# Two hybrid decoder layers: two weight column pairs exchanged, and the S5 states given to the output matmul as two VectorE products

## What is computed

```python
z = h @ w_in[l]                       # columns: s5_u, s5_gate, mla_cq, mla_ckv, mla_kr, ...
lam_bar = exp(lam * dt)
bu = einsum('blgh,gph->blgp', ug, b_bar)
state = linear_scan(lam_bar, bu)      # complex, along the tokens
y = einsum('blgp,ghp->blgh', state, c_c).real + d * ug
```

## Time and profile before

| | |
|---|---|
| runs before | 2877.06 us median of 3 (2876.66 to 2879.03) |
| profiled execution | 2878.85 us, span 2877.1 us, mean granted clock 0.993 |
| TensorE busy | 2804.0 us, 97% |
| VectorE busy | 1992.2 us, 69% |
| ScalarE busy | 1571.8 us, 55% |
| GpSimd busy | 745.6 us, 26% |
| HBM traffic | 183 GB/s over the span |

### The profile page before, as it was taken

How to read it: one execution, slowest core, us unless ns; L and a number is a source line. 1 busy time by engine, 2 the same in 40 slices (tenths; PEclk the granted TensorE clock), 3 DMA queues, 4 the chain that set the end, 5 groups by cost and what they waited for, 6 DMA issues and landing times.

```text
span 2877.1 us, 55833 instructions
## 1 busy us (share of the span) xinstructions
PE 2804.0 (97%) x16152; PEld 2410.4 (84%) x16152; DVE 1992.2 (69%) x3284; ACT 1571.8 (55%) x2812; POOL 745.6 (26%) x813
## 2 busy tenths in 40 slices
PE   6999999999999999999999999999999999999997
PEld 4878888888888888888877888888888888888886
DVE  8799999755555567555577999986555555755555
ACT  5555555655566565444455555556566555644443
POOL 3255555300001023111123545551001010411111
PEclk9999999999999999999999999999999999999998
DMA  6765656655555556777746565656555555577775
GB/s 225 227 186 177 184 175 183 180 166 159 165 156 169 164 149 201 217 210 209 206 142 190 173 186 175 186 173 179 166 155 168 163 154 157 168 211 217 209 210 175
DMA packets 276413, 522.65 MB, mean 182 GB/s; under 512 B 30913, under 2 KB 33873, under 8 KB 275281
## 3 DMA queue, kind: packets, MB, share of 16 engines
q1 hardware_dynamic: 257360, 477.13, 56.0%
q10 hardware_dynamic: 18944, 44.18, 4.8%
HBM read 508.60 MB, written 16.78 MB: 183 GB/s over the span
## 4 chain that ended last, share of the span: by engine, by line
PE 45%; DVE 2%; issue 2%; ACT 1%; POOL 0%; DVEq 0%; ACTq 0%; POOLq 0%
PE ps L294 26%; PE ps L293 13%; PE ps L443 1%; DVE w L973 1%; PE ps L326 1%; PE ps L456 0%; PE ps L452 0%; PE ps L296 0%; DVE zb L1512 0%; PE ps L337 0%; DVE yy L1042 0%; PE ps L304 0%; PE ps L465 0%; PE ps L464 0%; ACT w L590 0%
## 5 line engine op out<-in xcount | busy, mean ns | idle before, releaser
L294 PE MATMUL ps<-hb,w 128*128 128x512 f32 x5824 | 2053.0, 396 | 7.3 <-POOL hb L1542 6.1
L973 DVE TENSOR_TENSOR w<-raw,w 128x512 fp32r<-128x512 f32 x1760 | 1290.0, 740 | 789.6 <-ACT w L590 780.5
L590 ACT ACTIVATE w<-raw 128x512 fp32r<-128x512 f32 x1760 | 1092.9, 628 | 1035.3 <-PE ps L294 1034.3
L293 PE MATMUL ps<-hb,w 128*128 128x256 f32 x5690 | 1623.9, 285 | 13.8 <-DVE w L973 12.7
L294 PEld LDWEIGHTS ps<-hb,w 128*128 128x128 f32 x5824 | 1092.8, 188 | 251.4 <-issue 6.7
L293 PEld LDWEIGHTS ps<-hb,w 128*128 128x128 f32 x5690 | 1076.6, 189 | 57.0 <-DVE w L973 28.4
L294 PE MATMUL ps<-gl,w 128*128 128x512 f32 x640 | 226.7, 395 | 0.0
L1693 POOL TENSOR_TENSOR nf<-zb 128x256 f32 (+1 forms) x60 | 51.9, 864 | 537.2 <-DVE zb L1480 531.7
L294 PE MATMUL ps<-w,hb 128*128 128x512 f32 x512 | 179.1, 393 | 0.0
L293 PE MATMUL ps<-gl,w 128*128 128x256 f32 x560 | 156.6, 280 | 0.0
L1546 POOL TENSOR_TENSOR sx<-yl 128x256 f32<-128x256 f32 x16 | 15.6, 975 | 504.2 <-DVE yl L1346 504.2
(11 more groups left out here) (299 smaller groups left out, 2470.1 us busy)
## 6 DMA issues: line engine op xcount, KB each, us to landing
raw<-in_w SPq DMA_DIRECT2D x1763, 256.0 KB, 2.8
mlaw<-in_mlaw ACTq DMA_DIRECT2D x16, 768.0 KB, 4.2
mlaw<-in_mlaw ACTq DMA_DIRECT2D x16, 512.0 KB, 3.5
gate<-xres ACTq DMA_DIRECT2D x32, 256.0 KB, 4.3
xres<-zb ACTq DMA_DIRECT2D x32, 256.0 KB, 3.6
zb<-in_x SPq DMA_DIRECT2D x8, 512.0 KB, 7.3
xres<-in_x SPq DMA_DIRECT2D x4, 1024.0 KB, 6.5
s5w<-in_s5w ACTq DMA_DIRECT2D x16, 256.0 KB, 2.7
```

The costliest lines, as they stand in the source:

```text
L293: mm(acc[:, T:], a_lo, m_hi, start=False, stop=False, skip_group_check=True)
L294: last = mm(acc, a_hi, m_both, start=(k == 0), stop=(k == nk - 1), skip_group_check=True)
L590: A(w2[:, d, :, 0, :], raw[:, s, :, :], ACT.Copy).then_inc(hi_ready, 1)
L973: V.tensor_tensor(w2[:, d, :, 1, :], raw[:, s, :, :], w2[:, d, :, 0, :].bitcast(F), ALU.subtract).then_inc(w2_ready, 1)
```

## The change

It does three things.
1. The host orders the weight columns otherwise: pair 1 now holds the latents and the light half, pair 2 the second 512 S5 columns. `one=True` moves from pair 2 to pair 1 on TensorE and ScalarE, and VectorE gets the destinations of both pairs as an argument.
2. `s5_back` writes its product into a buffer of its own, `turned[j]`, (two in `gate`, two in a new tile `qki`, which also holds the former tiles qd, ki, ke and yl). `s5_state` and GpSimd's `back` go; `s5_back2` on VectorE, at step 8j + 6, makes the other product. VectorE takes over GpSimd's wait for `state_used` ahead of part 0.
3. `s5_out` multiplies `cprime` by both products and adds all four in PSUM: 16 matmuls instead of 8.

```diff
+        qki = sb("qki", [P, 4, T])
+        qd, ki, ke, yl = (qki[:, i, :] for i in range(4))
...
+        turned = (gate[:, 0, :, :], gate[:, 1, :, :], qki[:, 0:2, :], qki[:, 2:4, :])
...
                 pe.wait_ge(s5_done, it + 1)
-                pe.wait_ge(state_ready, it * 4 + 5)
+                pe.wait_ge(tab_used, it * 4 + 5)
+                pe.wait_ge(back_ready, it * 4 + 5)
                 for a in range(2):
-                    for j in range(4):
-                        last = mm(ps[32 * j:32 * j + 32, B_Y, 0:T], cprime[:, a, j, :], states[j][:, a, :],
-                                  start=(a == 0), stop=(a == 1), skip_group_check=True)
+                    for n, part in enumerate((states, turned)):
+                        for j in range(4):
+                            last = mm(ps[32 * j:32 * j + 32, B_Y, 0:T], cprime[:, a, j, :], part[j][:, a, :],
+                                      start=(a == 0 and n == 0), stop=(a == 1 and n == 1), skip_group_check=True)
...
-                pre_pair(1, {29: lambda: s5_in(l * G8, 0)})
-                pre_pair(2, s5_steps(l * G8, first=True), one=True)
+                pre_pair(1, {29: lambda: s5_in(l * G8, 0)}, one=True)
+                pre_pair(2, s5_steps(l * G8, first=True))
...
-                dve.wait_ge(state_ready, it * 4 + (j + 1))
+                dve.wait_ge(scanned, it * 8 + (2 * j + 1))
...
             def s5_back(it, j):
 
-                dve.wait_ge(scanned, it * 8 + (2 * j + 2))
-                V.tensor_tensor(yy[:, :, :], g2[:, ::-1, :], tab[:, 1:3, :], ALU.mult).then_inc(tab_used, 1)
-
-            def s5_state(it, j):
-                dve.wait_ge(tab_used, it * 4 + (j + 2))
-                dve.wait_ge(back_ready, it * 4 + (j + 2))
-                V.tensor_tensor(states[j][:, :, :], states[j][:, :, :], yy[:, :, :], ALU.add).then_inc(state_ready, 1)
+                dve.wait_ge(scanned, it * 8 + (2 * j + 3))
+                if j == 0:
+                    dve.wait_ge(state_used, it + 1)
+                V.tensor_tensor(turned[j], g2[:, ::-1, :], tab[:, 1:3, :], ALU.mult).then_inc(tab_used, 1)
+
+            def s5_back2(it, j):
+                V.tensor_tensor(states[j][:, :, :], g2[:, :, :], tab[:, 0:1, :].to_broadcast([P, 2, T]),
+                                ALU.mult).then_inc(back_ready, 1)
...
-                    for d, f in ((1, s5_rotate), (2, s5_rotate2), (3, s5_sum), (4, s5_scan), (5, s5_back), (7, s5_state)):
+                    for d, f in ((1, s5_rotate), (2, s5_rotate2), (3, s5_sum), (4, s5_scan), (5, s5_back), (6, s5_back2)):
...
-                pre_pair(2, s5_steps(l * G8, 0, first=True), one=True)
+                pre_pair(2, s5_steps(l * G8, 0, first=True),
+                         dst=(zb[:, Z_S5 + 4:Z_S5 + 6, :], zb[:, Z_S5 + 6:Z_S5 + 8, :]))
...
-            def back(it, j):
-
-                pool.wait_ge(scanned, it * 8 + (2 * j + 2))
-                if j == 0:
-                    pool.wait_ge(state_used, it + 1)
-                G.tensor_tensor(states[j][:, :, :], g2[:, :, :], tab[:, 0:1, :].to_broadcast([P, 2, T]),
-                                ALU.mult).then_inc(back_ready, 1)
...
                 turns(it, 1)
                 s5_cprime(it)
-                back(it, 0)
                 turns(it, 2)
-                back(it, 1)
                 turns(it, 3)
-                back(it, 2)
...
-                back(it, 3)
...
-    pre = np.concatenate([s5u, cq[:, :CC], kr, glr, pad, qk, lruu, cq[:, CC:], ckv, gv[:, :3 * CC]], axis=1)
+    pre = np.concatenate([s5u[:, :2 * CC], cq[:, :CC], kr, glr, pad, s5u[:, 2 * CC:], qk, lruu, cq[:, CC:], ckv, gv[:, :3 * CC]], axis=1)
```

More of the change, by code:

```diff
@@ L110, in trunk @@
         us = sb("us", [P, T])
-        yl = sb("yl", [P, T])
         kv = sb("kv", [P, 2, T])
@@ L119, in trunk @@
         lg = sb("lg", [P, 2, T])
-        qd = sb("qd", [P, T])
-        ki = sb("ki", [P, T])
-        ke = sb("ke", [P, T])
+        qki = sb("qki", [P, 4, T])
+        qd, ki, ke, yl = (qki[:, i, :] for i in range(4))
         attm = sb("attm", [P, 2, P])
@@ L173, in trunk @@
         cprime_ready, nf_ready, tab_ready = sem("cprime_ready"), sem("nf_ready"), sem("tab_ready")
-        bu_ready, bu_read, tab_used, state_ready, state_used = (sem("bu_ready"), sem("bu_read"), sem("tab_used"),
-                                                                sem("state_ready"), sem("state_used"))
+        bu_ready, bu_read, tab_used, state_used = (sem("bu_ready"), sem("bu_read"), sem("tab_used"),
+                                                                sem("state_used"))
         xc_ready, ri_ready, lru_act, yl_ready, yl_squared = (sem("xc_ready"), sem("ri_ready"), sem("lru_act"),
@@ L697, in _ @@
                 pre_pair(1, {0: [lam_exponent], 2: [turn_sines], 25: [lambda: s5_inputs(l * G8, 0)],
-                             31: [lambda: s5_tables(l * G8, 0)]})
+                             31: [lambda: s5_tables(l * G8, 0)]}, one=True)
                 own.restart()
-                pre_pair(2, s5_steps(l * G8, 0), one=True)
+                pre_pair(2, s5_steps(l * G8, 0))
                 own.restart()
@@ L1077, in _ @@
             dve.sem_inc(s5_done, 1)
-            dve.sem_inc(state_ready, 1)
+            dve.sem_inc(scanned, 1)
+            dve.sem_inc(back_ready, 1)
             C1 = 6.28125
@@ L1251, in _, with pre_pair @@
                 own.restart()
-                def pre_pair(i, steps, one=False):
+                def pre_pair(i, steps, dst=None):
                     for c in range(CH_PAIR):
@@ L1259, in pre_pair @@
                             h = c // CH_HALF
[L1260 to L1265, removed]
+                            z = zb[:, bass.ds(i * 4 + 2 * h, 2), :] if dst is None else dst[h]
+                            evac(h_l + (i * 2 + h), h, z, z.shape[1])
+                pre_pair(1, {0: [s5_turns], 4: [s5_scale], 6: [s5_scale2], 14: [lru_softplus]},
+                         dst=(zb[:, Z_LATENT[0]:Z_LATENT[0] + 2, :], kg.unsqueeze(1)))
                 own.restart()
-                pre_pair(2, s5_steps(l * G8, 0, first=True), one=True)
+                pre_pair(2, s5_steps(l * G8, 0, first=True),
+                         dst=(zb[:, Z_S5 + 4:Z_S5 + 6, :], zb[:, Z_S5 + 6:Z_S5 + 8, :]))
                 own.restart()
@@ L1536, in _ @@
             own.restart()
-            pool.sem_inc(back_ready, 1)
             def split_lo(k, count, dst=hb):
```

## The result

The changed kernel takes **2884.58 us** (median of 10 runs, 2883.81 to 2885.42) against 2877.22 us before (10 runs, 2876.07 to 2879.03): +7.4 us, a ratio of 1.0025, 95% interval 1.0017 to 1.0034. By that interval it is slower, where I had forecast 2875.0 us and a range up to 2881. The profiled execution took 2883.92 us (span 2882.1); the one of before lay 1.6 us above its median, so the two traces differ by 5.1 us only.

What follows compares the result with a forecast made beforehand. TensorE was taken to bound the kernel, with its waits for VectorE's low parts. The terms -20.4 + 3.0 + 1.0 + 14.3 = -2.1 us, against the median 2877.06 us, gave 2875.0 us, range 2869 to 2881.

Steps and rivals of the forecast that it cites:

- What bounds the kernel: TensorE, busy 97% of the span, waiting 13.2 us for VectorE's low parts; other engines' time counts only where TensorE waits.
- The pairs exchanged, and the new light half: Moving the light half (16 one-tile weight chunks) to pair 1 saves 20.4 us; stalls and loads there cost 3.0 and 1.0.
- the stalls: In pair 1's light half, low parts late behind VectorE's softplus chain: two stalls, 0.85 and 0.45 us; +3.0 us, two layers.
- the loads: In pair 1's light half, weight loads late, partly behind the first layer's 1 MB copy of x: +1.0 us, between 0 and 4.
- The rival of a light half that starves on loads: Pair 1's second half held up by raw loads, losing the old 10 us again: 2891 us; chance 0.10.
- the 358 GB/s of the prediction: HBM-to-core limit from the Trainium skill: 0.73 us a chunk, light half 0.5 us late by bandwidth alone; sum unchanged.
- Eight more matmuls: s5_out going from 8 to 16 matmuls adds four slots, 0.89 us, for each of 16 groups: +14.3 us on TensorE.
- On the path that is 0 us: Moving GpSimd's product to VectorE saves VectorE about 54 us and GpSimd some 120, but gains nothing on the path.
- the forecast "same": Whole kernel: -2.1 us, to 2875.0 us, within the 5.8 us that a measurement can't tell from no change; chance 0.57.
- The waits moved: ScalarE's tables wait for VectorE's step 6, about as early or earlier; VectorE's low parts behind its wait for state_used are safe.
- The one for a slower end: The rival that pair 1's light half starves on loads: 2891 us; chance 0.10.
- The one for dearer matmuls: Rival at s5_out: a gap up to 0.33 us a group between product sets, 5 us, 2880 us; slower only above +8, 0.04.

Runs made afterwards that it cites:

- the exchange alone: The kernel before with only the light half moved from pair 2 to pair 1 and the matching host column order: 2861.81 us, ratio 0.9943.
- the squares held back: The changed kernel, but GpSimd waits for the layer's last S5 product before it begins the squares of the latents: 2878.48 us, ratio 0.9999 to the kernel before.
- the cleared version: The exchange alone, with softplus moved to the middle stage and the third and fourth 1 MB copies of x issued 16 loads later: 2859.11 us, ratio 0.9936.
- the products alone: The kernel before with only the two separate products and 16 output matmuls, pairs not exchanged: 2895.91 us, ratio 1.0062.
- the doubled s5_out: The kernel before with each of s5_out's 8 matmuls issued twice, nothing else: 2893.36 us, ratio 1.0051.
- the split s5_out: The changed kernel with the squares held back, and s5_out as eight matmuls behind chunk 1 and eight behind chunk 2: 2878.88 us, ratio 1.0004 to the kernel before.

## Why the prediction was wrong, by its own steps

**What bounds the kernel: right.** TensorE and its waits for the low parts; VectorE's 64 us and GpSimd's 124 us, given back, bought nothing. TensorE's waits for the low parts were foreseen at 3 to 6 us in total and measured 8.4, of which 4.4 us stand in the second half of the two middle stages.

**The pairs exchanged, and the new light half: right.** -20.4 + 3.0 + 1.0 = -16.4 us was the sum; the exchange alone measured 16 us. That it agrees so closely is in part luck: the stalls held (0.82 and 0.22 us measured, 0.85 and 0.45 foreseen), but the loads, taken at 1.0 us, cost TensorE no wait, and the two light halves of the changed kernel are 1.8 and 2.0 us over the 12.30 instead of 1.5, 0.8 us more together that no term named. The load behind the copy made TensorE wait only once softplus was gone. The rival of a light half that starves on loads fell: in the changed kernel ScalarE waits for loads 0.21 us at 116.37 us and 1.27 us at 118.27 us, at the end of the half, but TensorE waits for neither, and the granted clock stayed at 1.00. Nor did the 358 GB/s of the prediction bound the loads: from 114 to 120 us they ran at 372 GB/s on average, in layer 1 at 381 from 1534 to 1540 us. (Stretches of the changed kernel's light half: busy us and count of PE, PEld, DVE, ACT, POOL, then clock, DMA share, GB/s.)

```profile
110.00:112.00 2.00, 2.00 (x13) 1.76 (x12) 1.95 (x4) 1.78 (x4) 0.00 (x0) 1.00 0.96 324
...
116.00:118.00 2.00, 2.00 (x14) 1.51 (x14) 1.57 (x3) 0.79 (x2) 0.00 (x0) 1.00 1.01 353
```

**Eight more matmuls: the mechanism right, the size short.** Slots 0.86 us against 0.89 predicted, but behind a block of 16 the chunks keep the slow pace that the block of 8 had ended, 0.30 us more in a steady pair. By the halves s5_out costs a layer 6 x 1.17 us in pairs 3 to 8 and, with the squares held back, 0.9 and 0.7 us in the middle stage, some 17 us for both; the time from the exchange alone to the whole change with its squares held back is 16.7 us. Predicted: 14.3. This term alone would have left the time inside the range. No gap stands between the two sets, as the even slots of the earlier trace rows had it.

**"On the path that is 0 us": the step that failed.** The products' move to VectorE was costed at nothing with the cover named as TensorE, "which waits nowhere in steady pairs". The prediction knew that the two engines slow each other and held that this costs nothing; I asked what VectorE and GpSimd gain, and which waits move, but not what GpSimd does next with the time. Its two last products were also its brake: each waits for a scan of the last S5 group, and the ten latent squares stand behind them in its queue. Without them the squares start 17 us early and run beside the layer's last S5 group, which they used to follow. The last group of a layer is not a steady pair. Cost: 3.6 us a layer by the halves; 6.1 to 7.5 us of the time, by the run that holds them back.

**The sum again, by the halves of both layers, changed kernel against before:** -14.2 us for the four halves from pair 1's second to pair 3's first (with their s5_out), +11.7 for ten more steady first halves, +1.8, +7.1 and +0.5 for the first, second and third half of the middle stage: +6.9 us. Measured by the medians: +7.4. The two profiled executions differ by 5.1 us only; the 1.8 us between lie outside these halves and have no cause that I know. Without the squares the forecast "same" holds (2878.5 us, inside the range); with them the time lies outside it.

**The waits moved: right.** VectorE nowhere waits for s5_out, and the tables' wait costs nothing with the squares held back. **The rivals:** none named the squares. The one for a slower end put it into the loads. The one for dearer matmuls had up to 5 us for a gap; 2.9 us came, by the pace and not by a gap.

## What to carry to other kernels

When work is taken from an engine that is off the critical path, follow that engine's queue past the removed instructions to the next thing it will start, and ask what this then runs beside: a removed instruction may have been the wait that kept two engines apart. A light stretch of the bounding engine belongs where its feeders have nothing else to do, and moving it was worth 16 to 19 us here without any instruction saved. Work that an engine with time to spare does should not be taken off it at the price of matmuls on the busy one: 64 us less on VectorE, 4 us for each of the 16 groups, were paid with 1.17 us of TensorE a steady group.

## What the runs showed that I had not expected

TensorE's stream of weight chunks has two paces at the same granted clock, 1.39 and 1.41 us a chunk. In the steady pairs of every trace here the two chunks ahead of s5_out run at 1.42 us; a block of 8 matmuls was followed by 1.39 us there, a block of 16 by 1.41 us, whatever its order and buffers. But it is no law of the block: the exchange alone (pair 3 of layer 1) and the cleared version (pair 3 of layer 0, pair 4 of layer 1) have 1.39 us ahead of 8 matmuls and 1.41 behind, and the products alone (pair 3 of layer 0) and the doubled s5_out (pair 4 of layer 1) have 1.39 us on both sides of 16 matmuls. In the steady pairs and in these five places a block of 16 left the pace as it was and a block of 8 changed it. That is no law either: the second block of the split s5_out changed nothing, and in pair 3 of layer 1 of the doubled s5_out, one chunk after a wait of TensorE, the pace goes from 1.39 us ahead of 16 matmuls to 1.42 behind.

Elsewhere the pace shifts between neighbours: pair 0's second half and pair 1's first take 22.19 and 22.61 us in layer 0 before and with the change, and 22.61 and 22.19 us with the squares held back, 44.80 us in each, though nothing in them differs. Where it does not even out it costs time: second half and next first half take 23.82 + 24.99 us instead of 23.51 + 24.70 in layer 1 of the exchange alone, 0.6 us. That is one reason why sums of small differences between two traces don't close to better than about 1 us.
